# A two-layer diffusion trunk with mixture of experts: earlier state and kept loads, the first projection by halves, and gate and up by halves in the expert turns

## The reference

```python
mod = silu(cond) @ w_ada[l] + b_ada[l]              # 1024 x 6144: shift, scale, gate, twice
hn = rmsnorm(x, norm_mix[l]) * (1 + sc1) + sh1
proj = hn @ w_in[l]                                 # 1024 x 3840, cut into 12 column blocks
o = concat(diff_attention(...), bidir_retention(...), bidir_hgrn2(...))
x = x + g1 * (o @ w_out[l])                         # 1024 x 1024
hn = rmsnorm(x, norm_ffn[l]) * (1 + sc2) + sh2
# mixture of 16 experts, router shared by the layers: best group of 4, then the top 2 in it
act = silu(hn @ w_gate[l, e]) * (hn @ w_up[l, e])   # 1024 x 512 each, e = 0..15
x = x + g2 * sum_e gate_e * (act @ w_down[l, e])    # 512 x 1024
```

## Time and profile before

| | us |
|---|---|
| median of two runs | 916.56 (915.92 and 917.2) |
| profiled execution | 919.49 |
| its span, first to last instruction | 917.6 |
| PE busy in the span | 872.9 (95%) |
| DVE, ACT, POOL busy | 454.6, 171.0, 79.4 |
| data moved | 307.37 MB, mean 335 GB/s |
| turns of the first layer, from the first gate matmul | from 256.91 |
| turns of the second layer, from the gather | from 690.55 |

### The profile page before, as it was taken

How to read it: one execution, slowest core, us unless ns; L and a number is a source line. 1 busy time by engine, 2 the same in 40 slices (tenths; PEclk the granted TensorE clock), 3 DMA queues, 4 the chain that set the end, 5 groups by cost and what they waited for, 6 DMA issues and landing times.

```text
span 917.6 us, 13378 instructions
## 1 busy us (share of the span) xinstructions
PE 872.9 (95%) x4762; PEld 446.0 (49%) x4766; DVE 454.6 (50%) x845; ACT 171.0 (19%) x444; POOL 79.4 (9%) x110
## 2 busy tenths in 40 slices
PE   4899999989899999999999999999989999999997
PEld 1655566558743333333337455756874333333332
DVE  2395887753563323322236987876356332333222
ACT  2202015231411111110121201442231111110011
POOL 1113130000010000000011223000001000000001
PEclk9999999999999999999999999999999999999999
DMA  8997565768789999999997555474558999999993
GB/s 361 412 397 312 229 233 228 312 237 352 286 315 424 422 423 423 422 424 424 424 413 308 216 223 198 190 286 196 235 219 331 422 424 422 424 423 422 423 425 138
DMA packets 50317, 307.37 MB, mean 335 GB/s; under 512 B 8682, under 2 KB 8698, under 8 KB 16848
## 3 DMA queue, kind: packets, MB, share of 16 engines
q1 hardware_dynamic: 42368, 291.52, 78.0%
q0 software_dynamic: 4848, 12.39, 3.6%
q10 hardware_dynamic: 3040, 2.62, 0.9%
HBM read 305.45 MB, written 4.73 MB: 338 GB/s over the span
## 4 chain that ended last, share of the span: by engine, by line
PE 75%; DMA 15%; DVE 5%; ACT 2%; issue 1%; SPq 1%; DVEq 0%; ACTq 0%
PE ps L484 71%; DMA ring<-in_w_experts 10%; PE ps L519 3%; DMA wT<-in_w_in 3%; DMA ring<-in_w_ada 2%; ACT eP L1755 1%; DVE hnT L1221 1%; PE ps L551 1%; ACT hnT L1827 1%; DVE rt L1167 1%; SPq L397 0%; DVE eP L1477 0%; DVE eP L1475 0%; DVE x L1738 0%; DVE proj L1340 0%
## 5 line engine op out<-in xcount | busy, mean ns | idle before, releaser
L484 PE MATMUL ps<-ring,proj 128*64 128x512 f32 x1024 | 285.1, 596 | 1.8 <-ACT proj L2017 1.7
L484 PE MATMUL ps<-ring,hnT 128*128 128x512 f32 (+1 forms) x576 | 204.2, 505 | 4.3 <-DVE t L1566 2.3
L484 PEld LDWEIGHTS ps<-ring,proj 128*64 128x64 f32 x1024 | 86.8, 137 | 137.8 <-issue 136.2
L484 PEld LDWEIGHTS ps<-ring,hnT 128*128 128x128 f32 x576 | 106.5, 191 | 78.2 <-issue 70.3
L1722 DVE COPY proj<-ps 128x512 f32<-128x512 f32 x16 | 11.1, 692 | 122.9 <-PE ps L484 122.9
L484 PE MATMUL ps<-home_qc,proj 128*64 128x512 f32 x128 | 57.8, 594 | 3.2 <-DMA ring<-in_w_experts 3.2
L484 PE MATMUL ps<-ring,silT 128*32 128x512 f32 x384 | 46.8, 608 | 14.1 <-DMA ring<-in_w_ada 7.1
L484 PE MATMUL ps<-home_kd,proj 128*64 128x512 f32 x128 | 57.6, 593 | 0.0
L484 PE MATMUL ps<-home_ra,proj 128*64 128x512 f32 x128 | 57.6, 592 | 0.0
L1708 DVE RECIPROCAL proj<-proj 128x512 f32<-128x512 f32 x16 | 53.7, 3353 | 0.6
L1707 DVE TENSOR_SCALAR proj<-proj 128x512 f32<-128x512 f32 x16 | 6.8, 427 | 84.9 <-ACT proj L1755 84.9
(11 more groups left out here) (288 smaller groups left out, 1073.5 us busy)
## 6 DMA issues: line engine op xcount, KB each, us to landing
ring<-in_w_experts SPq DMA_DIRECT2D x128, 1024.0 KB, 17.6
ring<-in_w_ada SPq DMA_DIRECT2D x48, 1024.0 KB, 9.4
ring<-in_w_in SPq DMA_DIRECT2D x24, 1024.0 KB, 8.2
home_qc<-in_w_experts SPq DMA_DIRECT2D x16, 1024.0 KB, 15.8
home_ra<-in_w_experts SPq DMA_DIRECT2D x16, 1024.0 KB, 19.7
home_kd<-in_w_experts SPq DMA_DIRECT2D x16, 1024.0 KB, 21.2
ring<-in_w_out SPq DMA_DIRECT2D x8, 1024.0 KB, 10.8
eP<-in_w_experts SPq DMA_DIRECT2D x4, 1024.0 KB, 10.4
```

Source lines behind the costliest of these rows:

```text
L484: ins = nc.tensor.matmul(*a, **k)
```

## The change

The change has six parts.

1. In the turns, PE does the first row halves of gate and up, then the second halves, and the expert weights are stored in that order. In turn 0 half of the gather of the second half is put between the first halves of gate and up.
2. In layer 0, block f is done by row halves: `by_half` does all heads and groups with `eP`, then all with `wT`, into two banks. The modulation steps behind the blocks are shifted later (the sum is the same), and the loads with them.
3. `end_state(1, "h")`, ACT's copy of it and its store are moved from the way to the experts to a place ahead of `da_weights(1, 1)`, in bank 4.
4. SP loads the kept pieces of `home_kc` and `home_es` ahead of four ring slots and `xy`.
5. The copy of block s, group 0, goes from DVE to ACT; the router's three DVE instructions go behind two of the residual steps; three of the zero matmuls are replaced by four others at an earlier place.
6. At the end, POOL does both additions of group 0 and DVE both of group 1; before, each did one half of each group.

```diff
-ADA_BEHIND = ((2, 3, 3, 3, 3, 2, 4, 4), (0, 0, 3, 3, 3, 2, 0, 0))
+ADA_BEHIND = ((0, 2, 3, 3, 4, 4, 4, 4), (0, 0, 3, 3, 3, 2, 0, 0))
...
                 first_loads(("ro", 1), slots=(HOME["ra"], HOME["kd"]))
+                keep("kc", ("hstate",), ("rstate",))
+                keep("es", ("mixed", 0), ("mixed", 1), ("stored",), ("stored_state",))
                 first_loads(slots=TURN_ORDER[l][7:9])
                 keep("xy", ("x1", 1))
                 first_loads(slots=TURN_ORDER[l][9:])
-                keep("kc", ("hstate",))
                 keep("hn", ("rows", 1, 1))
-                keep("es", ("mixed", 0), ("mixed", 1), ("stored",), ("stored_state",))
...
+                def by_half(name, b):
+
+                    ss, banks = [], [b]
+                    for half in range(2):
+                        ss.append(slot(RING + half))
+                        for p in range(2):
+                            if p and not half:
+                                banks.append(next_bank())
...
+                            for g in range(NG):
+                                if not p:
+                                    wait_for_input(g, half)
+                                for hl in range(2):
+                                    h = 2 * p + hl
+                                    for k in range(KH * half, KH * (half + 1)):
+                                        for d in range(2):
+                                            col = 64 * h + 256 * d
+                                            last = mm(ps[64 * d:64 * d + 64, banks[p], 256 * hl + P * g:256 * hl + P * (g + 1)], by_k(ss[half], 512)[:, k % KH, col:col + 64], hnT[:, k, tok(g)], start=False, stop=(k == KC - 1), skip_group_check=True)
...
-                ss = open_block("f")
-                by_head_and_group("f", 0, ss, b)
-                by_head("f", 1, ss)
+                    by_half("f", b)
...
                 modulation_by_feature(l, 1, next(turn_of_banks))
+                end_state(1, "h", T_GI, 4)
                 da_weights(1, 1)
...
                 normalized_group("hn2", "xn2", 1)
-                end_state(1, "h", T_GI)
...
+                for b in range(4, 8):
+                    mm(ps[:, b, :], zeros[:, 0:P], zeros[:, 0:BLK], start=False, stop=False, skip_group_check=True)
                 copied_group("hn2", 1)
...
-                stream_zeros(2, 3)
...
-                    gather()
+                    gather(0, range(KH))
+                    gather(1, range(KH // 2))
...
-                        for i in range(2):
-                            pe.wait_ge(S(f"bank{2 + i}_free"), c.claim(2 + i))
-                            for half in range(2):
-                                if not t and not i and half:
+                        for half in range(2):
+                            for i in range(2):
+                                if not half:
+                                    pe.wait_ge(S(f"bank{2 + i}_free"), c.claim(2 + i))
+                                if not t and not half and i:
+                                    gather(1, range(KH // 2, KH))
...
-                                pair = [turn_slot(t, 4 * i + 2 * half + e) for e in range(2)]
+                                pair = [turn_slot(t, 4 * half + 2 * i + e) for e in range(2)]
...
-                            owed.append(pair[1])
-                            last.then_inc(c.fills(2 + i, "gu", i), 1)
+                                if half:
+                                    owed.append(pair[1])
+                                    last.then_inc(c.fills(2 + i, "gu", i), 1)
                             if t >= SPREAD_FROM:
-                                scatter(t - 1, i, range(NG - i))
+                                scatter(t - 1, half, range(NG - half))
...
-                evac_block("s")
                 da_norm(1, 0)
...
-                st(tt(router_scaled, wrt, modT[:, 3, :, 1:2].broadcast_to([P, KC, NE]), ALU.mult), "router_scaled")
...
-                for n in range(4):
+                for n in range(2):
+                    first_residual(n, 0)
+                st(tt(router_scaled, wrt, modT[:, 3, :, 1:2].broadcast_to([P, KC, NE]), ALU.mult), "router_scaled")
...
+                for n in range(2, 4):
                     first_residual(n, 0)
...
-                squares_of(4, 16, "dao", 1, 0)
+                squares_begun(4, "dao", 1, 0)
+                evac_block("s", 0)
+                squares_ended(4, 16, "dao", 1, 0)
+                end_state(1, "h")
```

More of the change, by code:

```diff
@@ L666, in by_head_and_group @@
                     last.then_inc(c.fills(b, "projP", name, p), 1)
+                def by_half(name, b):
[6 more added lines that the diff above has]
+                            if not half:
+                                mm(ps[:, banks[p], :], zeros[:, 0:P], zeros[:, 0:BLK], start=True, stop=False, skip_group_check=True)
+                            for g in range(NG):
[7 more added lines that the diff above has]
+                                            last = mm(ps[64 * d:64 * d + 64, banks[p], 256 * hl + P * g:256 * hl + P * (g + 1)], by_k(ss[half], 512)[:, k % KH, col:col + 64], hnT[:, k, tok(g)], start=False, stop=(k == KC - 1), skip_group_check=True)
+                                            if not (half and g and hl and k == KC - 1 and d):
+                                                pay(last)
+                            if half:
+                                last.then_inc(c.fills(banks[p], "projP", name, p), 1)
+                    owed.extend(ss)
                 def queries_by_head_pair(ss):
@@ L1020, in _, with gather @@
                     led.found[((led.where, 0), "seat", 0)] = ("seat", led.where, 0)
-                    def gather():
+                    def gather(half, tiles):
                         led.turn = 0
-                        pe.wait_ge(c.of("seat", 0), c.at("seat", 0))
-                        for half in range(2):
+                        if not tiles[0]:
                             pe.wait_ge(S(f"bank{half}_free"), c.claim(half))
-                            for k in range(KH):
-                                for g in range(NG):
-                                    last = mm(ps[:, half, k * P:(k + 1) * P], rows[:, g, KH * half + k, :], seat[:, g, :], start=(g == 0), stop=(g == 1))
-                                    if not (k == KH - 1 and g):
-                                        pay(last)
+                        for k in tiles:
+                            for g in range(NG):
+                                last = mm(ps[:, half, k * P:(k + 1) * P], rows[:, g, KH * half + k, :], seat[:, g, :], start=(g == 0), stop=(g == 1))
+                                if not (k == KH - 1 and g):
+                                    pay(last)
+                        if k == KH - 1:
                             last.then_inc(c.fills(half, "xT", half), 1)
@@ L1733, in _ @@
                         dve.wait_ge(S(c.last[0]), c.last_value())
-                    if g and l + 1 < L:
+                        if g and l + 1 == L:
+                            half = slice(h * BLK, (h + 1) * BLK)
+                            st(tt(x[:, g, half], x[:, g, half], to, ALU.add), "x2", h)
+                    if l + 1 == L:
+                        continue
+                    if g:
                         c.l, led.where = l + 1, f"L{l + 1}"
@@ L2090, in second_residual @@
                 c.l, led.where = l, f"A{l}"
+                if l + 1 == L:
+                    for h, product in enumerate((first_product[0], nsq[:])):
+                        half = slice(h * BLK, (h + 1) * BLK)
+                        pool.wait_ge(c.of("x2p", 0, h), c.at("x2p", 0, h))
+                        put(g_.tensor_tensor(x[:, 0, half], x[:, 0, half], product, ALU.add), "x2a", h)
+                    return
                 for g in range(NG):
```

41 lines of the change are left out of this document (25 added, 16 removed).

## The result

| | kernel before | kernel after |
|---|---|---|
| median | 916.56 us (915.92 to 917.2, 2 runs) | 933.92 us (932.5 to 935.34, 2 runs) |
| ratio, 95% interval | | 1.0189 [1.0116, 1.0263] |
| profiled execution, span | 919.49, 917.6 | 932.5, 930.7 |

The kernel is slower by 17.4 us, 1.9%, inside the forecast range (909 to 936) and twice the forecast step of 8.6.

What follows compares the result with a forecast made beforehand. PE, busy 95% of the span, was taken to bound the kernel. Turns +22.2 and clock +2.8, less gains of 5.2, 1.7, 2.9, 2.1, 4.2 and 0.3, gave +8.6: 916.56 to 925 us, range 909 to 936.

Steps and rivals of the forecast that it cites:

- brackets in the turns: PE waits before the transposes for the chain behind gate: 11.1 us a layer, +22.2 us for both.
- falls of the clock in the turns: One fall of PE's granted clock, 1.4 us, in each turn 0: +2.8 us, bounds 0 and 22.
- waits for weights: PE's waits of 3.2 us in the turns and 2.0 at the change of layer should go: -5.2 us.
- block f by halves: Layer 0's block f starts near 31.5, not 33.23, and queries end at 66.5 against 71.01: -1.7 us, bounds 0 and -3.4.
- end of the layer: Waits before the attention weights shrink by 0.9 in each layer, plus layer 1's clock fall: -2.9 us, bounds -0.5 and -3.5.
- output projection: PE's wait of 1.18 for DVE behind the router instructions shrinks by 1.05 in each layer: -2.1 us, bounds 0 and -2.4.
- way to the experts: Without end_state there the gather comes earlier: -3.1 in layer 0, -1.1 in layer 1, together -4.2 us, bounds -1 and -5.5.
- the end: At the kernel's end the first group no longer waits for DVE: -0.3 us.
- The bare chain is half as long: Rival, 20%: turns 4 to 7 pay 0.9, turns 1 to 3 nothing, no clock falls; 911 us.
- the turns cost nothing: Rival, 5%: weights set the pace, so PE's new waits lie in time it would have waited anyhow; 900 us.
- The gains before the turns don't come: Rival, 15%: PE meets its gains again as waits for gates and router, half of 11.2 lost; 931 us.
- the rule of the Trainium skill: Frequent short pauses between matmul groups can keep the clock going back and forth; taken for every turn, the upper bound.

Runs made afterwards that it cites:

- e3: The kernel after with the scatter matmuls gathered behind up's second half in turns 1 to 7; 912.35 us, ratio 0.9936.
- e4: The kernel after without the reciprocal behind gate, a constant 0.5 in place of the sigmoid (another function); 908.03 us, ratio 0.9893.
- e1: The kernel after with the turns alone put back (gate whole, then up whole, gather in one piece, old weight layout); 907.36 us, ratio 0.9886.
- e2: The kernel before with the new order of the turns alone, its gather and weight layout included; 943.77 us, ratio 1.0277.
- e6: e1 with the loads of the two kept pieces behind the ring's, as in the kernel before; 908.36 us, ratio 0.9891.
- e10: e6 with the store of HGRN2's state also issued where the kernel before issues it; 911.25 us, ratio 0.9925.
- e5: e1 with block f of layer 0 whole and that layer's modulation steps where the kernel before has them; 907.62 us, ratio 0.9883.
- e9: e1 with four matmuls of zeros ahead of each of the two groups of router matmuls before the experts; 910.02 us, ratio 0.9907.
- e11: e1 with DVE's three router instructions ahead of the first residual, as in the kernel before; 908.55 us, ratio 0.9900.
- e12: The kernel after, unchanged, timed again in five more runs; 935.18 us, ratio 1.0175.

## Why the prediction was right in its sign and short in its size

| step of the forecast | forecast | shown |
|---|---|---|
| brackets in the turns | +22.2 | +21.1, and +3 beyond the brackets, some 0.2 a pause |
| falls of the clock in the turns | +2.8 | +4.7 on the mean, all places together, at most |
| waits for weights | -5.2 | -5.2 |
| block f by halves | -1.7 | 0 (one trace each; 0.1) |
| end of the layer | -2.9 | 0 (0 to -0.6 a layer) |
| output projection | -2.1 | -2.1 |
| way to the experts | -4.2 | -4.1 (-3 to -5 by the falls counted) |
| the end | -0.3 | 0 |
| sum | +8.6 | +17.4 |

**The turns.** This step held almost to the tenth: the forecast brackets were 1.69, 0.84 and 2.66, the measured ones 1.60, 0.73 and 2.75. e3 and e4 show the mechanism from both sides: lengthen the cover or shorten the chain, and the bracket goes. Missing was that a pause costs about 0.2 beyond its bracket; this is worked out from the spacing of the turns, in e1 and in after. "The bare chain is half as long" and "the turns cost nothing" have fallen. "The gains before the turns don't come" has come true in size, though I gave it 15%: of the 11.2 that I counted there and at the end, 4.9 are missing.

**The clock.** The mean granted clock of the 33 runs of before is 0.9948, or 4.8 us of its span, and that of the 7 runs of after 0.9899, 9.5 us; the difference is 4.7 where I took 2.8. It is an upper bound: in every profile 0.3 to 1.9 us of it are lost behind PE's last matmul, where PE has nothing left to do, and where PE waits anyway a fall costs less (below). I put one fall in each turn 0; the eight turns 0 with the long bracket have nine, each of 1.7 where I took 1.4. The second place, ahead of the experts, had none in layer 1 of before and two in after.

My reason for so few was weaker than it read. I took from the earlier trace rows that the waits of 0.82 and 1.5 had brought no fall, but a slice there is 23 us long and still shows 9 with one fall in it, as it does at 34, 242 and 629 us. The windows of before settle it, for this one execution:

```profile
272.00:277.00 5.00, 3.77 (x20) 1.91 (x22) 1.79 (x5) 0.59 (x1) 1.02 (x1) 1.00 1.01 425
476.00:481.00 5.00, 3.20 (x26) 1.29 (x28) 3.17 (x8) 1.65 (x4) 0.23 (x1) 1.00 1.05 417
```

The falls did not come in all turns: the rule of the Trainium skill that I named (TensorE: Matmul & The Clock Gate, A second HAM failure mode) is not borne out by the pauses of 0.7 and 1.6 us once every 27 or 28, whose windows all stand at 1.00. Turn 5 of layer 0 in after:

```profile
408.00:413.00 5.00, 3.40 (x17) 1.60 (x18) 2.93 (x7) 0.58 (x1) 0.00 (x0) 1.00 1.02 428
```

**The waits for weights.** The size was right and its reason only in part. In after the 11 us more on PE are reason enough, as e2 shows. Without them the kept loads do nothing (e6); the store of the state, named in one sentence of the forecast, brings back 2.2 of the 3.2 in e10's profile. The 2.0 at the change of layer went because after comes there later: e1 has 1.9 of them again.

**Block f by halves** is one of the two steps that failed. The forecast of its course was close (start 31.19, `diagonal` at 66.92 behind a wait of 1.61, as against 31.5, 66.5 and 1.7). But the row that I measured it against, 71.01, held a fall of the clock of 1.7. My -1.7 is that fall and nothing else: less the fall, before is at 69.3 and after at 66.9 with 2.8 of steps still to do. The earlier start (2.0) is met again as the wait of 1.6 for DVE at `diagonal`. Nor does the change do away with the fall for good. The three profiles with the block whole (before, e2, e5) all have it, but three of the eleven with halves have one just ahead of the block (e9, e11, e12), and the six runs of before with a mean clock of 0.999 (0.9 us lost in all) have room for none.

**The end of the layer** is the other. Of the -0.9 in each layer, 0.7 was to come from DVE, freed of the copy, and DVE's last product there (L1464) is indeed 0.7 earlier in layer 1, counted from the transposes of PE in front of it. But PE doesn't keep it. `end_state` takes 0.84 of the waits (1.40 in layer 0, 1.70 in layer 1), and a wait that I had not seen stands behind the attention weights, for ACT's copy of them (L1806):

```profile
632.76 0.66 PE L519 MATMUL ps<-c_begin,eP 128*128 128x128 f32 x4 [0.36 <-DVE xs L1464]
...
634.40 3.70 PE L484 MATMUL ps<-ring,hnT 128*128 128x512 f32 x8 [0.46 <-ACT wT L1806]
```

With 0.63 of such waits in layer 0 and 0.82 in layer 1, `end_state` and the waits take as long as the waits did. From block f of layer 1 to its output projection e2, with this part as before, takes 162.72 and after 162.60. In layer 0, from the attention weights at 157.65 and 156.20 to the output projection, before takes 47.55 and e1 47.44. And 1.1 of the 2.9 was again a fall of the clock in one profile.

**Output projection and way to the experts** were right together, and the way in part by luck. Before has a fall of 1.7 there in layer 0:

```profile
242.50:247.50 5.00, 4.56 (x25) 3.64 (x23) 3.97 (x27) 2.65 (x8) 0.00 (x0) 0.66 1.01 428
```

Less that, from one to the first gather it is 46.25 in before and 43.70 in e1 in layer 0, and 45.66 against 41.95 (43.65 less 1.7 in e1) in layer 1: 6.3 in all, as forecast. But a fall doesn't cost its full 1.7 here: after, with one fall in layer 0, takes 44.40, only 0.7 more than e1 with none. Counted so, layer 1 gains 2.7 and the sum is 5.3; with one fall on both sides (before 47.95 and after 44.40 in layer 0, e2 47.28 and e1 43.65 in layer 1) it is 7.2. Either way the two layers gain about the same, where I had 4.15 and 2.15: my -3.1 for layer 0 held the fall of the row that I started from, my -1.1 for layer 1 was too small, and the two errors cancel. No run puts `end_state` back by itself, so its part of the gain is argued.

With the right column the sum is 17.4. It comes from rows and means of different runs, and its agreement with 933.92 - 916.56 is luck in part: against the 33 runs the step is 16.1 (1.75%), and the terms of the clock and of the way to the experts are each uncertain by 1 to 2 us.

## What to carry to other kernels

Before two products are interleaved by halves, write down what has to run behind the end of the first one and what is left to hide it: here moving gate's end behind up's first half took away 3.5 us of cover and paid 21 us for it, while the 3 us of waits for weights go without it too (0.3 left in e1). Work that is moved into a wait is still work in its new place: book its leaving, and of the wait only what is left over once the next engine in the chain has been looked at. And before a stage of one profile is compared with a forecast, look in windows of a few us for falls of the clock and take them out of it.

## What the runs showed of the hardware that was not expected

- The granted clock falls to 0.50 of full, 1.2 GHz, for a stretch (window 685 to 690 of after) in which 1.7 us or twice that are lost, in places that differ from run to run of one kernel. In the 33 runs of the kernel before in the experiments, the six with a mean clock of 0.999 took 915.7 to 917.0 us, the four with 0.992 took 920.2 to 921.0. The mean clock accounts for some 70% of the spread of its times (variance), at 0.5 us for each us lost: where PE waits anyway, or has nothing left to do, a fall costs less or nothing.
- It fell also where PE had had no wait over 0.4 us for 30 us, behind 16 matmuls of 16 columns (32 records) ahead of the experts (the window at 687 of after). Behind waits of 2.75 us in turn 0 it fell in seven of eight cases, behind 0.8 to 0.9 in one of twenty. Zeros put into the wait of 2.75 us gave back 2 to 3 us without changing the result.
- A pause of PE costs some 0.2 us more than the bracket in the timeline, of which 0.1 to 0.15 can be the modelled end of the matmul before it.
- With weights arriving at 422 to 425 GB/s (e10's page, slices of the turns) and PE without pauses, a reload that starts 2.2 us later (e10) is felt 150 us later, in waits of 1.6 and 0.6 us at 410 and 438; nothing on the way makes it up in layer 0. In layer 1, where a fall of the clock lies around the gather, no such wait came.
